# GpSimd adds the squares of a head's two tiles ahead of the mean product, in cross attention's keys and queries

## What is computed

```python
def rms_norm_2(x, g, eps=NORM_EPS):
    xf = x.astype(jnp.float32)
    y = xf * lax.rsqrt(jnp.mean(xf * xf, axis=-1, keepdims=True) + eps)
    return (y * g.astype(jnp.float32)).astype(x.dtype)

def cross_attn(xn, mn, wq, wkv, q_gain, k_gain, wo):
    ...
    q = rms_norm_2((xn @ wq).reshape(B, S, CA_HEADS, CA_HEAD_DIM), q_gain, QK_EPS)
    kv = (mn @ wkv).reshape(B, M, 2, CA_HEADS, CA_HEAD_DIM)
    k = rms_norm_2(kv[:, :, 0], k_gain, QK_EPS)
    v = kv[:, :, 1]
    s = jnp.einsum('bshd,bmhd->bhsm', q, k).astype(jnp.float32) * (CA_HEAD_DIM ** -0.5)
    p = jax.nn.softmax(s, axis=-1).astype(v.dtype)
    o = jnp.einsum('bhsm,bmhd->bshd', p, v).reshape(B, S, CA_HEADS * CA_HEAD_DIM)
    return o @ wo
```

## Time and profile before

| what | value |
|---|---|
| median of 3 runs | 2026.48 us (2022.93 to 2030.1) |
| the profiled execution's own time | 2025.92 us |
| its span in the profile | 2024.1 us |
| TensorE matmul busy | 1949.9 us, 96% of the span |
| TensorE weight load busy | 1527.9 us, 75% |
| VectorE busy | 1133.5 us, 56% |
| ScalarE busy | 800.1 us, 40% |
| GpSimd busy | 450.7 us, 22% |
| mean granted TensorE clock | 0.994 of full speed |

### The profile page before, as it was taken

How to read it: one execution, slowest core, us unless ns; L and a number is a source line. 1 busy time by engine, 2 the same in 40 slices (tenths; PEclk the granted TensorE clock), 3 DMA queues, 4 the chain that set the end, 5 groups by cost and what they waited for, 6 DMA issues and landing times.

```text
span 2024.1 us, 31665 instructions
## 1 busy us (share of the span) xinstructions
PE 1949.9 (96%) x13058; PEld 1527.9 (75%) x13058; DVE 1133.5 (56%) x1810; ACT 800.1 (40%) x1369; POOL 450.7 (22%) x537
## 2 busy tenths in 40 slices
PE   8989999999999988879999989999999999999999
PEld 6857888888866767867787865578887778888887
DVE  5354544444576866759455766645365456666432
ACT  4264432232446532335225467743244443232211
POOL 0552000000302657643100057712230110000000
PEclk9999999999999999999999999999999999999999
DMA  5202322222224220002275100033232222222222
GB/s 180 89 22 84 104 94 94 94 94 94 94 91 156 83 74 4 4 13 85 95 202 182 63 32 1 1 131 98 80 130 73 73 94 94 94 94 94 96 88 87
DMA packets 46733, 174.91 MB, mean 86 GB/s; under 512 B 5071, under 2 KB 5455, under 8 KB 45824
## 3 DMA queue, kind: packets, MB, share of 16 engines
q1 hardware_dynamic: 43488, 154.35, 22.8%
q0 software_dynamic: 3104, 18.56, 2.8%
HBM read 166.53 MB, written 10.55 MB: 87 GB/s over the span
## 4 chain that ended last, share of the span: by engine, by line
PE 87%; ACT 5%; DVE 3%; POOL 2%; issue 2%; DMA 0%; SPq 0%; POOLq 0%; ACTq 0%; DVEq 0%
PE ps L358 23%; PE ps L359 22%; PE ps L363 22%; ACT arena L1611 2%; PE ps L2791 2%; PE ps L1073 2%; PE ps L1492 2%; PE ps L2799 2%; PE ps L1779 1%; PE ps L1461 1%; PE ps L1508 1%; PE ps L1936 1%; PE ps L2144 1%; PE ps L3498 1%; POOL arena L3143 1%
## 5 line engine op out<-in xcount | busy, mean ns | idle before, releaser
L340 ACT ACTIVATE w_hi<-wring 128x1024 fp32r<-128x1024 f32 (+1 forms) x267 | 280.1, 1050 | 574.4 <-PE ps L363 552.2
L344 DVE TENSOR_TENSOR w_lo<-wring,w_hi 128x1024 fp32r<-128x1024 f32 (+1 forms) x267 | 332.6, 1246 | 204.0 <-ACT w_hi L340 201.7
L358 PE MATMUL ps<-ffn_input_hi,w_hi 128*128 128x512 f32 x352 | 139.5, 396 | 0.0
L359 PE MATMUL ps<-ffn_input_hi,w_lo 128*128 128x512 f32 x352 | 139.1, 395 | 0.0
L1657 POOL TENSOR_TENSOR arena<-arena 128x512 f32<-128x512 f32 (+3 forms) x160 | 113.6, 733 | 30.5 <-DVE arena L1561 25.5
L358 PE MATMUL ps<-gate_input_hi,w_hi 128*128 128x512 f32 x256 | 106.0, 414 | 4.1 <-DVE w_lo L344 2.5
L358 PE MATMUL ps<-mlp_input_hi,w_hi 128*128 128x512 f32 x256 | 101.6, 397 | 0.0
L358 PE MATMUL ps<-mlp_hi,w_hi 128*128 128x512 f32 x256 | 101.2, 395 | 0.0
L359 PE MATMUL ps<-gate_input_hi,w_lo 128*128 128x512 f32 x256 | 101.2, 395 | 0.0
L359 PE MATMUL ps<-mlp_input_hi,w_lo 128*128 128x512 f32 x256 | 101.2, 395 | 0.0
L359 PE MATMUL ps<-mlp_hi,w_lo 128*128 128x512 f32 x256 | 101.2, 395 | 0.0
(11 more groups left out here) (485 smaller groups left out, 4545.4 us busy)
## 6 DMA issues: line engine op xcount, KB each, us to landing
wring<-weights SPq DMA_DIRECT2D x276, 512.0 KB, 3.5
bias_wide_scratch<-bias_line_scratch POOLq DMA_DIRECT2D x1, 4096.0 KB, 25.2
arena<-bias_wide_scratch POOLq DMA_DIRECT2D x1, 4096.0 KB, 19.2
wring<-weights SPq DMA_DIRECT2D x9, 384.0 KB, 2.9
arena<-x_t SPq DMA_DIRECT2D x4, 512.0 KB, 8.5
xn_scratch<-arena POOLq DMA_DIRECT2D x1, 2048.0 KB, 6.8
x_scratch<-arena POOLq DMA_DIRECT2D x1, 2048.0 KB, 9.5
arena<-xn_scratch POOLq DMA_DIRECT2D x1, 2048.0 KB, 8.8
```

The costliest lines, as they stand in the source:

```text
L340: act.activation(self.w_part(self.w_hi, m), self.split_source(m), ACT.Copy).then_inc(self.w_hi_ready, 1)
L344: eng.tensor_tensor(self.w_part(self.w_lo, m), self.split_source(m), self.w_part(self.w_hi, m).bitcast(F32), ALU.subtract).then_inc(self.s ...
L358: pe.matmul(out, hi[:, c, :], src.hi[:, src.place(at + c), :], start=(at + c == 0), stop=False)
L359: pe.matmul(out, lo[:, c, :], src.hi[:, src.place(at + c), :], start=False, stop=False)
```

## The change

GpSimd adds the two squared tiles of a head in place, into the slot of the first, as soon as both are there, and TensorE takes the mean of the sum with one product where it took two. It holds for the keys (128x256) and the queries (128x512) of cross attention, 4 heads each. Another user of the query class, with one tile per mean, keeps its products. The additions stand in GpSimd's program in the stages `pk` and `pq3`. The semaphore that GpSimd raises comes from a pool of semaphores shared by name with a base count (`Signal`), and the self attention's semaphores are moved to that pool too; its waits and instructions stay the same in number.

```diff
+class Signal:
+    def __init__(self, k, name, total):
+        self.sem, self.base = k.common(name), k.reserve(name, total)
+
+    def wait(self, eng, n):
+        eng.wait_ge(self.sem, self.base + n)
...
+class SquareSums:
+    def __init__(self, k, first, outs, span, n):
+        self.k, self.first, self.outs, self.span, self.n = k, first, outs, span, n
+        self.summed = Signal(k, "squares_summed", outs // 2) if span == 2 else None
+
+    def gpsimd(self, pool):
+        k = self.k
+        for a in range(self.outs // 2 if self.span == 2 else 0):
+            left, right = (k.square[:, (2 * a + r) % 4, 0:self.n] for r in range(2))
+            pool.wait_ge(k.square_ready, self.first + 2 * a + 2)
+            pool.tensor_tensor(left, left, right, ALU.add).then_inc(self.summed.sem, 1)
+
+    def total(self, pe, a):
+        k = self.k
+        if self.span == 2:
+            self.summed.wait(pe, a + 1)
+        else:
+            pe.wait_ge(k.square_ready, self.first + a + 1)
+        return k.square[:, self.span * a % 4, 0:self.n]
...
 class ProjectNorm(Stage):
...
+    def gpsimd(self, pool):
+        self.squares.gpsimd(pool)
...
                 k.open_acc(pe, t)
-                for r in range(self.span):
-                    j = i - self.span + r
-                    pe.wait_ge(k.square_ready, self.sq0 + j + 1)
-                    mm = pe.matmul(k.acc(t)[:, 0:self.n], k.const(self.mean), k.square[:, j % 4, 0:self.n],
-                                   start=(r == 0), stop=(r == self.span - 1))
-                mm.then_inc(k.acc_full, 1)
+                pe.matmul(k.acc(t)[:, 0:self.n], k.const(self.mean), self.squares.total(pe, i // self.span - 1),
+                          start=True, stop=True).then_inc(k.acc_full, 1)
```

More of the change, by code:

```diff
@@ L151, in __init__ @@
         self.bank_waits = {}
+        self.commons = {}
         self.n_used = 0
@@ L163, in sem, with common @@
         return self.ctx.enter_context(self.nc.semaphore(name))
+    def common(self, name):
+        if name not in self.commons:
+            self.commons[name] = self.sem(name)
+        return self.commons[name]
     def take_acc(self, n=1):
@@ L1405, in __init__ @@
         self.acc0, self.aux0 = k.n_acc, k.n_aux
[L1406 to L1417, removed]
         self.pair, self.t_order, self.t_at, self.t_count = [], [], {}, [0, 0]
@@ L1429, in __init__ @@
                 pairs += units[f].last
+        self.s_full = Signal(k, "scores_full", NT * len(units))
+        self.s_drained = Signal(k, "scores_drained", 2 * NT * len(units))
+        self.p_ready = Signal(k, "probs_ready", NT * len(units))
+        self.inv_ready = Signal(k, "inverse_ready", NT * len(units))
+        if units[0].gate is not None:
+            self.gated = k.sem("inverse_gated")
+        self.scaled = Signal(k, "probs_scaled", 2 * NT * len(units))
+        self.t_full = [Signal(k, f"probs_t_full{e}", self.t_count[e]) for e in range(2)]
+        self.t_drained = [Signal(k, f"probs_t_drained{e}", self.t_count[e]) for e in range(2)]
+        self.pv_done = Signal(k, "values_done", len(units))
+        self.out_drained = Signal(k, "out_drained", pairs)
     def place_t(self, key, e):
@@ L1437, in wait_out @@
     def wait_out(self, eng, pair):
-        eng.wait_ge(self.out_drained, pair + 1)
+        self.out_drained.wait(eng, pair + 1)
     def score_bank(self, u, e, i):
@@ L1457, in scores @@
         if u + back >= 0:
-            pe.wait_ge(self.s_drained, 8 * (u + back) + 2 * RANK[row] + 2)
+            self.s_drained.wait(pe, 8 * (u + back) + 2 * RANK[row] + 2)
         for e in range(2):
@@ L1469, in open_t @@
             e, count = self.t_order[n - 3]
-            pe.wait_ge(self.t_drained[e], count + 1)
+            self.t_drained[e].wait(pe, count + 1)
         return self.t_bank(key)
@@ L1486, in probs_t @@
             p = self.b.p[u % 2][e]
-            pe.wait_ge(self.scaled, 8 * u + 2 * (RANK[2] if part == 2 else RANK[1]) + e + 1)
+            self.scaled.wait(pe, 8 * u + 2 * (RANK[2] if part == 2 else RANK[1]) + e + 1)
             out = self.open_t(pe, (u, e, part))
@@ L1500, in values @@
         for e in range(2):
-            pe.wait_ge(self.t_drained[e], self.t_at[u, e, 0][1] + 1)
+            self.t_drained[e].wait(pe, self.t_at[u, e, 0][1] + 1)
         if h.compressed is not None:
@@ L1607, in exps @@
         for e in range(2):
-            act.wait_ge(self.s_drained, 8 * u + 2 * RANK[i] + e + 1)
+            self.s_drained.wait(act, 8 * u + 2 * RANK[i] + e + 1)
             at, c = slice(TRI[i], TRI[i] + P * (i + 1)), slice(2 * i + e, 2 * i + e + 1)
@@ L1618, in move_compressed @@
         if u >= 1:
-            act.wait_ge(self.pv_done, u - 1)
-        act.wait_ge(self.t_full[0], self.t_at[key][1] + 1)
-        copy(self.b.ct, self.t_bank(key)[0:64]).then_inc(self.t_drained[0], 1)
+            self.pv_done.wait(act, u - 1)
+        self.t_full[0].wait(act, self.t_at[key][1] + 1)
+        copy(self.b.ct, self.t_bank(key)[0:64]).then_inc(self.t_drained[0].sem, 1)
     def scalar(self, act):
@@ L1649, in gpsimd @@
                 count = NT * u + RANK[i] + 1
-                pool.wait_ge(self.inv_ready, count)
+                self.inv_ready.wait(pool, count)
                 inv = b.inv[:, u % 2, 2 * i:2 * i + 2]
@@ L1764, in __init__ @@
         self.ready0 = k.reserve("xn", outs)
+        self.squares = SquareSums(k, self.sq0, outs, span, n)
     def wait_dst(self, eng, i):
         eng.wait_ge(self.k.xn_ready, self.ready0 + i + 1)
+    def gpsimd(self, pool):
+        self.squares.gpsimd(pool)
     def tensor(self, pe):
@@ L1917, in __init__, with gpsimd @@
         self.ready0 = k.reserve("xn", outs)
+        self.squares = SquareSums(k, self.sq0, outs, span, S)
     def wait_dst(self, eng, i):
         eng.wait_ge(self.k.xn_ready, self.ready0 + i + 1)
+    def gpsimd(self, pool):
+        self.squares.gpsimd(pool)
     def tensor(self, pe):
@@ L1932, in tensor @@
                 k.open_acc(pe, t)
[L1933 to L1938, removed]
+                pe.matmul(k.acc(t), k.const(self.mean), self.squares.total(pe, i // self.span - 1), start=True,
+                          stop=True).then_inc(k.acc_full, 1)
             if self.beside is not None:
```

32 lines of the change are left out of this document (15 added, 17 removed).

## The result

The changed kernel takes 2040.41 us in the median of 6 runs (2037.94 to 2044.41), the kernel before 2028.51 on the same chip: a ratio of 1.0061, 95% interval 1.0047 to 1.0076. By that ratio it is 12.4 us slower (9.5 to 15.4); the two medians alone differ by 11.9. Forecast were 10.7.

A forecast was written before the change was run, and what follows sets the result against it. TensorE, busy 1949.9 of 2024.1 us, was taken as the bound. First wait 6.0, query means -2.58, second wait 5.5, last mean -0.86 and clock 2.6 gave +10.7 us, so 2037 us; range 2031 to 2043.

The forecast's parts named there:

- The keys, even: End of keys: three shorter means save 1.29 us, the last key mean's exposed addition (1.3 us) eats it.
- The first wait, +6.0: First query tile: TensorE waits for eight `cross_input_lo` queued on GpSimd behind the last key addition; all following moves +6.0 us.
- The queries' means, -2.58: Queries: three means behind a next tile need one product, not two, saving 3 x 0.86 = 2.58 us.
- The second wait, +5.5: Filler after the last query tile: waits for four `memory_lo` behind GpSimd's fourth query addition, +5.5 us.
- The last mean, -0.86: Last query mean, behind the filler: one product fewer, its addition long done, saving 0.86 us.
- The clock, +2.6: TensorE behind both new waits: granted clock falls to 0.50, costing 1.3 us each, +2.6 us.
- The rival without waits: GpSimd makes low parts while an earlier addition waits, so only products count: -3.4 us, 2023; chance 0.04.

The follow-up runs named there:

- spare products: Changed kernel plus thirteen TensorE products of constants, results unused, ahead of the last key mean, five low-part waits and the filler; 1.0049 against the kernel before.
- the queries mixed: Changed kernel with only the queries' additions mixed on GpSimd with the memory's low parts, in the order their operands come; 1.0025 against the kernel before.
- the semaphores alone: Kernel before with only the change's shared semaphores in the self attention, all means two products, no GpSimd additions; 1.0006 against the kernel before.

## Why the prediction was right

Slower was forecast, by 10.7 us; the stretch grew by 11.7 and the time by 12.4. The forecast of 2037 stood on a median before of 2026.5; the one measured beside the change was 2028.5, which is 2 of the 3.4 us between 2037 and 2040.4. Both waits came where they were forecast. By its own steps:

- **The keys, even.** 32.67 became 32.33: 0.3 us better than even. The exposed addition took 1.15 us beside the weight conversion, where 1.3 was taken between 0.7 and 1.5.
- **The first wait, +6.0.** The first query tile grew by 5.90, with the keys 5.56 in all. That the size is so close is partly luck, as two errors offset each other. The eight low parts took 10.85 us where 12.06 was taken, and the last product that waits for one moved by 4.6 us only, counted from the first key product. From it to the second tile went 1.18 us where it was 0.23: at half clock, and with 0.38 us of wait for VectorE's first weight part of that tile, a price the prediction did not have. The 0.7 us taken for a low part beside a conversion did not come in this profile; in the two other runs with this wait it did (the last section has the row). TensorE's waits for low parts were forecast to add to some 6 us and add to 2.6: a third fall of the clock, behind the wait for the last key sum, was not in the prediction, and at half clock the 16 products with the high parts alone took 5.50 us where they had taken 3.82.
- **The queries' means, -2.58.** With the clock at 1.00 the same part of the stretch shrinks from 42.47 to 39.90: 2.57. In the change it is 42.47 again, since the half clock costs 2.58 there, as the spare products show.
- **The second wait, +5.5.** The way to the filler grew from 1.87 to 7.32, by 5.45.
- **The last mean, -0.86.** 4.57 became 3.74 where the clock held, 0.83.
- **The clock, +2.6.** Mis-sized: 2.58 behind the first wait and 1.55 behind the second, 4.1 in all, where 1.3 for each was taken. Both slow stretches were long ones, of some 6.8 us. The first began only as the wait ended; half of the second lay in the wait. These 1.5 us more, less the 0.4 of the first wait, are the 1 us by which the sum fell short. The size isn't fixed: with the queries mixed, where the first wait is left as it is, the slow stretch behind it lasted 3.4 us and that part of the queries took only 1.25 more than at full clock (41.15 and 39.90).

```profile
1506.60:1510.00 3.40, 3.36 (x8) 2.70 (x9) 0.18 (x1) 2.14 (x3) 0.00 (x0) 0.50 0.41 142
1510.00:1513.50 3.50, 3.50 (x16) 2.82 (x16) 1.04 (x1) 0.00 (x0) 0.00 (x0) 1.00 0.34 123
```

- **The step that was missing:** VectorE beside GpSimd. The prediction let the low parts slide to the end of the keys and asked only who reads them. VectorE's timeline of the changed kernel, the last head's root and scaling:

```profile
1500.66 1.57 DVE L447 TENSOR_TENSOR root<-root_y 128x256 f32<-128x256 f32 x1 [0.93 <-ACT root_y L440]
...
1505.13 2.79 DVE L1864 SCALAR_TENSOR_TENSOR arena<-arena,vecs_sb,root 128x256 f32<-128x256 f32 x2
```

  The weight part stands behind them. In the change itself it costs 0.4 us, as TensorE is waiting for the low parts anyway; once these come in time it decides, as two runs showed.

The rival without waits fell with the row that has low parts ready behind a waiting addition. The Trainium skill's rule (TensorE: Matmul & The Clock Gate, section on the array's architectural detail), that GpSimd is strictly first in, first out, agrees with it. The estimate from the Trainium skill's cycles per element (GPSIMD Engine Reference, section 3.1), 1.1 us for a 512-wide low part, stayed under the 1.36 measured. The Trainium skill (GPSIMD Engine Reference, section 8) says that GpSimd contends with VectorE instructions that have two SBUF inputs; the runs agree, with 0.43 and 1.37 us for one such operation, and this was the rule to weigh.

## What to carry to other kernels

GpSimd's program was a queue here: an operation added to an engine that is idle four fifths of the time still delayed everything behind it by its own wait. Ask of each added wait what stands behind it and when that was made until now. The queries' additions cost nothing once they stood in the order in which their operands come; the keys' in that order still cost 2.2 us in the stretch. Then ask what the moved work runs beside: work moved to another time meets other neighbours. And a wait of a few us on TensorE can be paid again at half clock, here with 1.25 to 2.58 us.

## What the runs showed of the hardware that was not expected

- VectorE's 256-column root operations take 0.43 us alone and 1.37 to 1.57 beside GpSimd's two-input low parts, while GpSimd is slowed little: a low part of the changed kernel took 1.26 to 1.48 us. Which of two neighbours is slowed isn't fixed. VectorE's two weight conversions around the first wait, in the timeline of the changed kernel:

```profile
1496.44 1.22 DVE L361 TENSOR_TENSOR w_lo<-wring,w_hi 128x1024 fp32r<-128x1024 f32 x1
...
1507.85 2.28 DVE L361 TENSOR_TENSOR w_lo<-wring,w_hi 128x1024 fp32r<-128x1024 f32 x1
```

  The first was running when GpSimd's addition began: it kept its 1.22 us, and the addition took 1.15. The second began beside a low part that was running and took 2.28. In the earlier trace rows, too, it is GpSimd's tile that is slow and the conversion that is not. In the run with the queries mixed both happen in turn: a conversion that began beside one low part, and the next low part, the last, that began beside the conversion (in the run with spare products these two took 2.29 and 2.24 as well).

```profile
1503.17 2.29 DVE L361 TENSOR_TENSOR w_lo<-wring,w_hi 128x1024 fp32r<-128x1024 f32 x1
...
1504.34 2.24 POOL L911 TENSOR_TENSOR cross_input_lo<-arena,cross_input_hi 128x512 fp32r<-128x512 f32 x1
```

  In all these rows the one that began later pays; no run was made to test that.
- A wait of 2.06 us on TensorE at the end of the keys, behind a stretch of full work, was followed by 3.3 us at a granted clock of 0.50; so was one of 1.7. The wait of 2.5 us behind a softmax that the kernel before has the earlier trace rows is in all eleven profiles, and the clock fell at it or just behind it in six: its length alone doesn't decide.
- Programs with the same work ahead of the keys came to them at 1460.8 to 1470.7 us, with 24 to 48 us at a granted clock of 0.50 on the way. Even one program's executions differ: the kernel before took 2022.9 to 2031.1 us beside the change. So the spans of two profiles can't tell a change of a few us; the stretch around the change can: it is 87.27 us in the kernel before and with the semaphores alone.
